# Rows of two fixed experts gathered by wide products, and the room of h given to every third expert's weights, in a hybrid trunk with a mixture of experts

## The reference

```
grp_prob = softmax(t @ wg + bg);  grp_idx = top 1 of the 4 groups
sel = logits of the 8 experts of that group;  top_i = top 2 of them
y_e = (silu(t @ w_gate[e]) * (t @ w_up[e])) @ w_down[e]
out = sum over the token's two experts of weight * y_e
```

## Time and profile before

| what | value |
|---|---|
| median of 3 runs | 1152.79 us (1151.55 to 1156.19) |
| the profiled execution's own time | 1151.86 us |
| its span | 1150.1 us |
| busy share of the span | PE 84%, DVE 42%, ACT 29%, POOL 12% |
| moved by DMA | 302.08 MB, mean 263 GB/s |
| experts' stage of layer 0, of layer 1 | about 309 to 585 us, 866 to 1143 us |

### The profile page before, as it was taken

One profiled execution on the slowest core, in us unless ns is written; L12 is line 12 of the kernel. 1 busy time (PEld: TensorE's weight loads), 2 busy tenths in 40 slices (PEclk: granted clock), 3 DMA queues, 4 the chain that ended last, 5 costly groups with the idle time before them and its releaser, 6 DMA issues.

```text
span 1150.1 us, 20717 instructions
## 1 busy us (share of the span) xinstructions
PE 970.8 (84%) x7674; PEld 646.0 (56%) x7674; DVE 487.3 (42%) x1271; ACT 332.5 (29%) x879; POOL 138.0 (12%) x193
## 2 busy tenths in 40 slices
PE   5899888999468788788879999998964887888887
PEld 3456655655345455455558888776543554555454
DVE  2079876521632333333430314685145332333334
ACT  3211353530522222221330101575132222222222
POOL 0400140000400010000010055000022100010000
PEclk8999999999679999988979999998976999999998
DMA  9999736772269999999873323100215799999993
GB/s 353 279 316 361 254 110 234 264 271 74 101 229 374 416 416 417 419 418 418 337 257 110 96 87 129 56 1 2 78 69 219 298 416 417 416 417 417 417 418 126
DMA packets 84913, 302.08 MB, mean 263 GB/s; under 512 B 5541, under 2 KB 34449, under 8 KB 68465
## 3 DMA queue, kind: packets, MB, share of 16 engines
q1 hardware_dynamic: 81584, 291.03, 65.4%
q0 software_dynamic: 2832, 8.61, 2.6%
q10 hardware_dynamic: 432, 1.57, 0.3%
HBM read 291.87 MB, written 9.32 MB: 262 GB/s over the span
## 4 chain that ended last, share of the span: by engine, by line
PE 51%; DMA 26%; DVE 14%; ACT 3%; issue 3%; SPq 1%; POOL 1%; POOLq 0%; DVEq 0%; ACTq 0%
PE banks L666 26%; DMA ring<-in_moe_w_up_dram 24%; PE banks L978 6%; PE banks L675 5%; DVE a L1508 5%; PE banks L1022 4%; PE banks L973 4%; DVE a L1443 2%; PE banks L704 2%; PE banks L1001 1%; DVE rt L1443 1%; SPq L561 1%; DMA bc<-in_moe_be_dram 1%; PE banks L949 1%; POOL bc L2041 1%
## 5 line engine op out<-in xcount | busy, mean ns | idle before, releaser
L666 PE MATMUL banks<-ring,hT 128*128 128x256 f32 (+1 forms) x720 | 153.9, 376 | 1.7 <-ACT hT L1164 1.6
L666 PEld LDWEIGHTS banks<-ring,hT 128*128 128x128 f32 x720 | 135.0, 191 | 21.3 <-DMA ring<-in_ev_w_in_dram 1.9
L1216 ACT ACTIVATE a<-banks 32x256 f32<-32x256 f32 (+1 forms) x208 | 88.3, 425 | 199.0 <-PE banks L1001 100.5
L1539 DVE SCALAR_TENSOR_TENSOR xT<-banks,mod,xT 128x128 f32<-128x128 f32 x352 | 118.7, 409 | 63.0 <-PE banks L1022 63.0
L1022 PE MATMUL banks<-a 128*128 128x384 f32 x352 | 134.0, 527 | 3.5 <-ACT a L1216 3.3
L1443 DVE TENSOR_TENSOR a<-a,banks 64x128 f32<-64x128 f32 (+1 forms) x64 | 21.7, 340 | 268.9 <-ACT a L1199 268.9
L666 PE MATMUL banks<-hT,ring 128*128 128x384 f32 x384 | 127.9, 493 | 1.6 <-ACT hT L1164 1.6
L978 PE MATMUL banks<-ring,a 128*32 128x128 f32 x2560 | 92.1, 304 | 43.1 <-DMA ring<-in_moe_w_up_dram 42.5
L978 PEld LDWEIGHTS banks<-ring,a 128*32 128x32 f32 x2560 | 80.5, 122 | 69.5 <-issue 68.4
L973 PE MATMUL banks<-ring,a 128*64 128x256 f32 x704 | 85.7, 398 | 25.5 <-DMA ring<-in_moe_w_up_dram 20.4
L666 PEld LDWEIGHTS banks<-hT,ring 128*128 128x128 f32 x384 | 73.1, 192 | 53.5 <-issue 3.8
(11 more groups left out here) (262 smaller groups left out, 1038.3 us busy)
## 6 DMA issues: line engine op xcount, KB each, us to landing
ring<-in_moe_w_gate_dram SPq DMA_DIRECT2D x64, 1024.0 KB, 8.7
ring<-in_moe_w_up_dram SPq DMA_DIRECT2D x64, 1024.0 KB, 10.8
ring<-in_moe_w_down_dram SPq DMA_DIRECT2D x64, 1024.0 KB, 10.3
ring<-in_ada_w_dram SPq DMA_DIRECT2D x44, 1024.0 KB, 8.4
ring<-in_od_w_qkv_dram SPq DMA_DIRECT2D x12, 1024.0 KB, 5.5
ring<-in_ev_w_in_dram SPq DMA_DIRECT2D x6, 1024.0 KB, 12.8
a<-sorted_rows SPq DMA_DIRECT2D x12, 512.0 KB, 6.8
a<-in_ada_w_dram SPq DMA_DIRECT2D x4, 1024.0 KB, 17.6
```

The costliest lines, as they stand in the source:

```text
L666: mm = pe.matmul(out, lhsT, rhs, start=(k == 0), stop=(k == len(pairs) - 1))
L1216: ins = act.activation(y_pair[q % BUFFERS][row:row + rows, width * b:width * b + width], work[3][rows * b:rows * b + rows, 0:width], ACT.Copy)
L1539: ins = ve.scalar_tensor_tensor(out=xT[:, c, a:b], in0=work_banks(l)[pair + k][:, a:b], scalar=mcol(l, 5, c, j), in1=xT[:, c, a:b], op0=AL ...
```

## The change

1. **Rows of experts 0 and 1 by products.** After the places, DVE works out for each token whether it belongs among the first 64 rows of a fixed expert, and at which row (three instructions of 128x6), and makes three 128x128 matrices `picks` of ones and zeros from a row of lane numbers (POOL's iota, cast by DVE) by three comparisons and three comparisons with addition. PE multiplies them with `htok`: two results of 128x512, three products each (`rows`). DVE and ACT copy one each to `fixed_rows`; PE turns them by eight transposes (`rowsT`); DVE and ACT copy one half each to `fixedT`. On PE `rows` stands ahead of `lead`, and `rowsT` between `lead` and `places`.
2. **Order of PE's work.** After `places`: gate and up of expert 0, then of expert 1; expert 0's turn and down; the three `codes` products; expert 1's turn and down; then the turns of the six sorted blocks; then gate and up of expert 2. DVE does the products `hidden(0)` and `hidden(1)` after the diagonals; ACT copies `codes` between expert 0's result and the turned product of expert 1. POOL cuts out rows from expert 2 on.
3. **Weights.** `hT` and `a1` become one tile of three slots, `h_and_rows`. Experts with n % 3 = 2 use it, the others the ring: nine slots, three experts.
4. **Order on DVE.** The sums of the pairs' experts (`R_ID1`) move into the wait for `rank`; the sums of the ranks move ahead of the comparison of counts. `EXPERT_BANKS_FROM` moves the banks.

```diff
+        h_and_rows = sb("h_and_rows", [P, AHEAD, SLOT])
+        hT = h_and_rows.rearrange("p k n -> p (k n)")[:, 0:KD * TOK].rearrange("p (c t) -> p c t", c=KD)
+        a1 = h_and_rows.rearrange("p k n -> p (k n)")[:, KD * TOK:]
...
+        def expert_slot(l, n, k):
+
+            return h_and_rows[:, k, :] if n % AHEAD == AHEAD - 1 else slot(expert_piece(l, n, k))
...
+                        if n >= AHEAD:
+
+                            sp.wait_ge(sem(used), AHEAD * t + (NE * l + n - AHEAD + 1))
+                        elif n < AHEAD - 1:
+                            free(expert_piece(l, n, k))
...
                 sp.wait_ge(sem("order_ready"), l + 1)
-                weights(BUFFERS, 0, True, (0, 1))
...
+                is_filled(sp, ("rows", l, 1))
+                weights(AHEAD - 1, 0)
+                weights(AHEAD, 0, (0, 1))
+                with sp.Fori(0, (NE - 2 - AHEAD) // AHEAD) as t:
+                    for n in range(AHEAD + 1, 2 * AHEAD + 1):
+
+                        weights(n, t, (0, 1))
+                        weights(n - 1, t, (2,))
...
+                pe.wait_ge(sem("picked"), l + 1)
+                is_read(pe, ("htok", l, NT - 1, 1))
+                for b in range(2):
+                    product(opened(("rows", l, b)), [(picks[:, t, :], htok[:, t, 512 * b:512 * b + 512]) for t in range(NT)], True)
                 out = opened(("lead", l))
...
+                for b in range(2):
+                    out = opened(("rowsT", l, b))
+                    for j in range(2):
+                        is_read(pe, ("rows", l, j))
+                    turn(out, [fixed_rows[:, c:D:KD] for c in range(4 * b, 4 * b + 4)])
                 out = opened(("places", l))
...
+                def fixed_and_turns():
+                    gate_up(1)
+                    for n in range(STATIC):
+                        await_hid(n)
+                        hid_turn(n)
+                        down(n)
+                        if n == 0:
+                            pe.wait_ge(sem("diagonals_ready"), l + 1)
+                            for i in range(NT):
+                                mm = pe.matmul(work[4 + i], ones[:, :], diagonals[:, 4 * i:4 * i + 4, :], start=True, stop=True)
+                                mm.then_inc(sem("codes_filled"), 1)
+                    pe.wait_ge(sem("pair_rows_ready"), NT * (l + 1))
+                    for i in range(PAIRS // P):
+                        pe.wait_ge(sem(f"sorted{i}_loaded"), 16 * (l + 1))
+                        if i > 1:
+                            pe.wait_ge(sem("sorted_by_vector"), PAIRS // P * l + i - 1)
+                            pe.wait_ge(sem("sorted_by_scalar"), PAIRS // P * l + i - 1)
+                        for b in range(2):
+                            for c in range(4):
+                                mm = pe.transpose(work[4 + 2 * (i % 2) + b][:, P * c:P * c + P], sorted_in[i][:, 4 * b + c:D:KD], ident[:, :])
+                            mm.then_inc(sem("sorted_turned"), 1)
...
+                silu(0)
+                load_overflow(act, l)
+                silu(1)
+                hid_copy(0)
+                y_copy(0)
+                for i in range(NT):
+                    act.wait_ge(sem("codes_filled"), NT * l + i + 1)
+                    act.activation(pair_rows[:, 512 * i:512 * i + 512], work[4 + i], ACT.Copy).then_inc(sem("pair_rows_ready"), 1)
+                hid_copy(1)
+                y_copy(1)
...
+                of_the_choices(m(M_RANK), R_RANK1)
...
+                link(ve.tensor_scalar(fixed, ranks, float(ROWS), float(FURTHER_CODE), ALU.is_ge, ALU.mult))
+                link(scaled(fixed, fixed, ranks, ALU.add))
+                link(scaled(fixed, fixed, ids, ALU.add))
+                for t in range(NT):
+                    ins = ve.tensor_scalar(picks[:, t, :], lane, fixed[:, t:t + 1], None, ALU.is_equal)
+                link(ins)
+                for t in range(NT):
+                    ins = ve.scalar_tensor_tensor(out=picks[:, t, :], in0=lane, scalar=fixed[:, NT + t:NT + t + 1], in1=picks[:, t, :],
+                                                  op0=ALU.is_equal, op1=ALU.add)
+                ins.then_inc(sem("picked"), 1)
```

More of the change, by code:

```diff
@@ L252, in psum_order @@
                 g.add(("counts", l), "v")
+        g.add(("rows", l, 0), "v")
+        g.add(("rows", l, 1), "s")
         g.add(("lead", l), "v")
+        g.add(("rowsT", l, 0), "v")
+        g.add(("rowsT", l, 1), "s")
         g.add(("places", l), "v")
[L255 to L261, removed]
+        g.add(("first", l), "v")
     for b in range(2):
@@ L568, in expert_loads @@
                 sp.wait_ge(sem("order_ready"), l + 1)
-                weights(BUFFERS, 0, True, (0, 1))
[L570 to L577, removed]
+                is_filled(sp, ("rows", l, 1))
[5 more added lines that the diff above has]
+                        weights(n - 1, t, (2,))
+                weights(NE - 1, 0, (0, 1))
+                weights(NE - 2, 0, (2,))
+                weights(NE - 1, 0, (2,))
                 def loads(j, e, i):
@@ new lines, in routing @@
+                out = opened(("first", l))
+                for b in range(2):
+                    is_read(pe, ("rowsT", l, b))
+                w = []
+                for k in range(2):
+                    pe.wait_ge(expert_sem(l, 0, k), expert_landed(l, 0, k))
+                    w.append(expert_slot(l, 0, k).rearrange("p (k n) -> p k n", k=KD))
+                for c in range(KD):
+                    for k in range(2):
+                        mm = pe.matmul(out[ROWS * k:ROWS * k + ROWS, 0:FF], fixedT[:, c, 0:ROWS], w[k][:, c, :],
+                                       start=(c == 0), stop=(c == KD - 1), tile_position=(0, ROWS * k))
@@ L955, in experts @@
+                mm.then_inc(sem("filled"), 1)
+                is_filled(pe, ("first", l))
+                pe.nop().then_inc(sem("gate_up_filled"), 1)
             def experts(l):
@@ L1037, in experts @@
                 load_overflow(pe, l)
-                for name in groups.names[at[0] - 8:at[0]]:
+                assert groups.names[at[0] - 1] == ("first", l) and (at[0] - 1 - EXPERT_BANKS_FROM[l]) % 8 != 1
+                for name in groups.names[at[0] - 8:at[0] - 1]:
                     is_read(pe, name)
-                for n in range(1, STEPS_AHEAD + 1):
+                fixed_and_turns()
+                for n in range(STATIC, STEPS_AHEAD + 1):
                     step(n)
@@ L1409, in _ @@
                     act.activation(dst, src, ACT.Exp).then_inc(sem("exp_given"), 1)
-                for i in range(NT):
-                    is_filled(act, ("codes", l, i))
-                    done(act.activation(pair_rows[:, 512 * i:512 * i + 512], psum(("codes", l, i)), ACT.Copy))
+                act.wait_ge(sem("cache_stored"), 32 * (l + 1))
                 experts(l)
@@ L1697, in routing @@
                 ve.tensor_scalar(at_place[0:NE, :], lead_of_place[0:NE, :], lead_col[0:NE, 0:1], None, ALU.is_equal).then_inc(sem("places_compared"), 1)
+                is_filled(ve, ("rowsT", l, 0))
+                done(ve.tensor_copy(fixedT[:, 0:4, :], psum(("rowsT", l, 0)).rearrange("p (c r) -> p c r", c=4)))
                 lead_row = lead[:, NE:2 * NE]
```

162 lines of the change are left out of this document (76 added, 86 removed).

## The result

The changed kernel takes 1136.95 us (median of 4 runs, 1135.79 to 1139.83) beside 1152.17 of the kernel before (4 runs): a ratio of 0.9874, 95% interval 0.9853 to 0.9895, so 15.2 us less. In a second series it took 1138.57 (6 runs) beside 1152.02, 0.9891 (0.9872 to 0.9911). Its profiled execution took 1135.79 us with a span of 1134.1; the forecast for that was 1140.9, in a range of 1130 to 1151.

The account below looks back on a forecast made before the run. The experts' weight stream, DMA full at 417 GB/s, bounds the kernel; only an earlier or gapless start helps. Gains of 5.5 us in each layer: 1151.86 - 11.0 = 1140.9, so 1141; range 1130 to 1151.

Parts of the forecast that it names:

- X: Layer 0: time expert 5's bytes begin to flow, put at 357.7; gain 363.2 - X, 5.5 us.
- The tails behind both streams are as before: Work after each layer's weight stream was taken as unchanged, adding nothing to the 11.0 us gain.
- Steps 1 to 4: Layer 0 before PE's gate and up: picks to 311.9, rows to 319.2, lead at 320.0, DVE's diagonals to 331.9, slots 323.7.
- rival D: order_ready after 328.7 leaves the third slot empty while DVE is late; ends as B or C; C with D 0.19.
- Step 5: Both fixed experts' gate and up on PE, 322.6 to 330.6, end before DVE is free for hidden(0): cover of 1.5 us.
- Steps 6 to 9: Layer 0: hidden, both downs, codes 9.0 us to 341.1; turns, then 349.7; expert 2's product to 355.0; clock loss to 356.0.
- step 9: PE's idle 1.5 to 2.2 us among hidden, downs and codes may lose the clock: half of 2 us added.
- step 8: Expert 2's product on PE after idleness, clock at 0.50: 5.32 us, against 3.67 at full clock.
- A: No gap: expert 2's product ends by 348.9, gain 2 x 12.6 = 25.2 us, 1126.7; chance 0.06.
- B: Slower: PE at half clock from picks to turns, 14.3 us, loss of 8.8 in each layer, 1169; chance 0.07.
- C: No change: hand-overs on the new path cost 3 to 5.5 us more in all, 1147 to 1152; with rival D 0.19.
- The ports: DVE and POOL share ports by turns: six picks would delay the scatter by at most 1.6 us, swallowed by the gap.

Follow-up runs that it names:

- experiment 11: The changed kernel as it is, run once more in a longer series: 1138.57 us (6 runs).
- experiment 10: The changed kernel with twelve identity transposes in each of PE's two waits at a layer's end, longer series: 1135.50 us, 0.9860 of before.
- experiment 4: The changed kernel with the six wide products for the fixed experts' rows made twice: 1145.38 us, 0.9934 of before.
- experiment 3: Turns-first: changed kernel with sorted blocks' turns, expert 0's down, expert 2's gate and up before codes and expert 1's down: 1124.78 us, 0.9770 of before.
- the third set alone: The kernel before with only the third set of weight buffers and the change's SP order; no picks, wide products or new PE order: 1136.73 us, 0.9862.
- experiment 5: The kernel before with twelve identity transposes in each of PE's two waits at a layer's end: 1148.93 us, 0.9985 of before without them.

## Why the forecast was right, and where it was not

**X and the sum.** The forecast took X = 357.7 and 5.5 us of gain in each layer, 11.0 in all. X was 357.1, and the stages gained 5.5 and 5.7, 11.2 in all (by the formula, layer 0 would have 363.2 - 357.1 = 6.1). The profiled execution came out 5 us lower than forecast (1135.79 against 1140.9), and this pair of profiles shows where: 5.6 + 5.7 in the stages, 2.6 + 2.5 at the layers' ends, less 0.4 between the layers, 16.0 in all. "The tails behind both streams are as before" is the step that failed: the profile of before had both ends at half clock wholly or in part, the changed kernel's none, and in experiment 11 the changed kernel itself had one. So that the median came out 4 us below the forecast is nothing the forecast had reckoned with. In the medians the change gains 2 to 4 us beyond the stages; how that divides between the ends and the open rest of experiment 10 isn't shown.

**Steps 1 to 4.** Picks ended at 311.88 (311.9); one comparison took 0.23 to 0.29 us (0.27). Rows took 7.89 us, not 7.2: weight loads of its passes start 0.85 us apart up to 316.36 and 0.42 apart from 317.09, so the full clock came some 5 us after the start, and I had allowed 4. DVE took `lead` up at 320.41 (320.0) and the diagonals ended at 332.18 (331.9). The price of nine us on the DVE chain was 9.3, and experiment 4 shows that it is a price: some 5 us more on PE in each layer made 8.4. The slots came at 323.77 (323.7), so rival D is out.

**Step 5.** Gate and up of expert 1 ended at 331.65, 1.0 later than forecast, since 1.52 us of issue stand ahead of it; in the program the load of the overflow's value into a register lies there. DVE's product for expert 0 began at 332.36: the cover held, with 0.7 us left.

**Steps 6 to 9.** Expert 1's down ended at 341.18 (341.1), expert 2's product began at 350.01 (349.7), took 5.36 (5.32) and ended at 355.37 (355.0). In layer 0 the loss of clock in step 9 (1 us) did not come: down took 1.94 after short waits, and `codes` 2.84, both at full clock. In layer 1 it came, and the one in step 8 did not: expert 0's down took 3.62 us (883.55) and expert 2's product 3.67 (901.37), so the way from the sorted blocks to expert 5's gate was as long in both layers (35.00 and 34.95). The sum had 1.65 us for the one and half of 2 us for the other; each layer paid one of the two, 1.7 us. That X was right to 0.6 us is in part luck: the 1 us too much stands against 0.4 too little on the rest of the path (355.37 against 355.0).

**Rivals.** A (1126.7) needed expert 2's product by 348.9; it came 6.5 later here, but experiment 3 reached it by order alone, at 1124.78. B and C did not come: the half clock after the picks lasted only through part of `rows` (of B's terms one down in layer 1 came true, 1.7 us), and the hand-overs of step 6 took the 9.0 us forecast.

**The ports.** Six picks on DVE beside POOL's issues cost little: the six scatters ran from 309.74 to 317.29, 7.55 us, before from 309.66 to 317.10, 7.44. By the rule of the Trainium skill (SBUF — State Buffer, "SBUF: two separate sides") the forecast's estimate was a delay of at most 1.6 us; 0.1 is what the trace shows.

**What the forecast did not take apart.** It took the change as one thing. In the change's order on PE its two parts pull in opposite ways: by the stages the third set gives 13 to 15 us and the wide products take 2 to 4 back, because `lead` waits for them and because the turns, which all later experts need, moved behind both fixed experts' downs and `codes`.

## What to carry to other kernels

Where DMA is full for the rest of a stage, count the bytes that can go out before the first freed slot is needed, and the time at which that slot comes free; the difference is the hole, and buffers and the order of work both close it. On the engine that frees the slot, put first what the freeing needs and last what only the results need: that order took another 12 us off the changed kernel's median. A part that only makes something earlier is worth a run of its own: here it left the median where the third set alone had it (1136.95 and 1136.73) until the order behind it was changed.

## What the runs showed of the hardware

The same product after the same waits ran at either clock in different executions: the last spread after 1.74 and 1.64 us of waiting took 8.53, 7.47 or 5.71 us. Within one execution expert 2's product took 5.36 us after 2.91 us of idleness in layer 0 but 3.67 after 2.69 in layer 1. One profile doesn't tell which a kernel has. With twelve transposes of no use in each wait the clock was full in all ten ends seen, and the last spread began no later for them (4.72 us after the last turn in experiment 5, 4.73 before); with them the runs of the turns-first kernel lay within 1.6 us (1118.12 to 1119.67) instead of 6.9 (1120.89 to 1127.81).

A stall of 2.7 to 3.5 us on PE, without a wait that the profile shows, came at one place in 8 of the 13 profiles, always with the same programs (three of them were profiled twice), and the twelve useless transposes per wait put it in for the kernel before and took it out for the changed one. So two kernels can differ by 2 to 3 us at a place that the change never touched.

With nine slots the median time from issue to landing of an expert's piece rose from 8.7 to 10.8 us to some 16 to 19, at the same 417 GB/s: a piece is sent for earlier and arrives no faster.
